# Later small loads, memory rows copied first, and a score bank and probability buffer per head in cross attention

## What is computed

```python
mods  = silu(c)     @ w_ada + b_ada          # shift and scale of the latent rows
cmods = silu(c_ctx) @ w_ada + b_ada          # the same for the context rows
h     = modulate(rmsnorm(x),   sh, sc)       # then h @ w_in: gates, keys, queries, values
h_ctx = modulate(rmsnorm(ctx), csh, csc)

m = rmsnorm(mem, mem_norm_g)                 # cross attention of the second block, 4 heads of 128
k, v = headnorm(m @ w_xk), m @ w_xv
q    = headnorm(rmsnorm(x, norm2_g) @ w_xq)
x    = x + softmax(q @ k.T * 128**-0.5) @ v @ w_xo
```

## Time and profile before

| | us |
|---|---|
| median of 3 runs | 1256.4 (1254.93 to 1256.63) |
| the profiled execution | 1256.11 |
| its span, first to last instruction | 1254.0 |
| TensorE busy | 1179.5 |
| VectorE busy | 409.3 |
| ScalarE busy | 321.7 |
| GpSimd busy | 30.5 |
| mean granted TensorE clock | 0.975 of full speed |

### The profile page before, as it was taken

The page is one execution under the profiler, slowest core; times in us unless marked ns, Lnnn a source line. Parts: engine busy times, 40 slices in busy tenths (PEclk is TensorE's granted clock), DMA queues, the critical chain, the costliest instruction groups (busy, mean ns, idle before and its releaser), DMA issues.

```text
span 1254.0 us, 16528 instructions
## 1 busy us (share of the span) xinstructions
PE 1179.5 (94%) x6732; PEld 874.2 (70%) x6732; DVE 409.3 (33%) x1018; ACT 321.7 (26%) x738; POOL 30.5 (2%) x54
## 2 busy tenths in 40 slices
PE   6999999999999989989999999889678979999997
PEld 5678888888878778765555555568556848887443
DVE  1424334212322221231111111216776422224545
ACT  2481010053422220142122111332554331000000
POOL 0000000000000011000000000032000000000000
PEclk9999999999999999999999999899879979999999
DMA  9923113213347873629999997534200404444530
GB/s 374 406 96 135 67 67 134 101 68 103 124 172 277 313 287 134 239 106 395 414 423 424 418 411 301 202 127 143 68 1 1 186 33 152 137 165 150 185 135 33
DMA packets 34361, 241.66 MB, mean 193 GB/s; under 512 B 3898, under 2 KB 4282, under 8 KB 6012
## 3 DMA queue, kind: packets, MB, share of 16 engines
q1 hardware_dynamic: 32640, 233.85, 47.7%
q10 hardware_dynamic: 1020, 4.06, 0.9%
q0 software_dynamic: 640, 2.90, 0.7%
HBM read 239.74 MB, written 1.05 MB: 192 GB/s over the span
## 4 chain that ended last, share of the span: by engine, by line
PE 87%; DVE 5%; ACT 3%; DMA 2%; issue 1%; SPq 1%; DVEq 0%; ACTq 0%
PE bank L1304 21%; PE bank L1331 11%; PE bank L1313 9%; PE bank L1694 9%; PE bank L2045 6%; PE bank L1717 5%; PE bank L1656 3%; PE bank L1665 3%; PE bank L1376 2%; DMA arena<-in_stream 2%; PE bank L1396 1%; PE bank L1566 1%; PE bank L1569 1%; PE bank L1514 1%; PE bank L2017 1%
## 5 line engine op out<-in xcount | busy, mean ns | idle before, releaser
L1304 PE MATMUL bank<-arena,ring 128*128 128x256 f32 x736 | 159.3, 379 | 0.0
L1304 PEld LDWEIGHTS bank<-arena,ring 128*128 128x128 f32 x736 | 139.8, 190 | 19.0
L1304 PE MATMUL bank<-hTl,ring 128*128 128x256 f32 x512 | 112.8, 379 | 0.0
L1304 PEld LDWEIGHTS bank<-hTl,ring 128*128 128x128 f32 x512 | 97.0, 190 | 16.9 <-issue 4.3
L691 ACT ACTIVATE arena<-bank 128x512 f32<-128x512 f32 x70 | 41.2, 601 | 235.9 <-PE bank L1304 211.4
L1331 PE MATMUL bank<-ring,arena 128*128 128x256 f32 x432 | 95.9, 379 | 1.0 <-ACT arena L1174 0.7
L1331 PEld LDWEIGHTS bank<-ring,arena 128*128 128x128 f32 x432 | 81.8, 190 | 12.6 <-ACT arena L1174 1.0
L1313 PE MATMUL bank<-ring,arena 128*128 128x256 f32 x384 | 86.6, 385 | 2.3 <-DVE arena L2354 2.2
L1313 PEld LDWEIGHTS bank<-ring,arena 128*128 128x128 f32 x384 | 73.6, 193 | 14.1 <-DVE arena L2354 2.6
L1694 PE MATMUL bank<-ring,arena 128*64 128x256 f32 x512 | 57.0, 381 | 0.0
L1313 PE MATMUL bank<-ring,hTl 128*128 128x256 f32 x256 | 56.9, 380 | 0.0
(11 more groups left out here) (503 smaller groups left out, 1684.9 us busy)
## 6 DMA issues: line engine op xcount, KB each, us to landing
ring<-in_stream SPq DMA_DIRECT2D x163, 1024.0 KB, 6.6
arena<-in_stream SPq DMA_DIRECT2D x38, 1024.0 KB, 9.0
hTl<-in_stream SPq DMA_DIRECT2D x9, 1024.0 KB, 7.8
hTc<-in_stream SPq DMA_DIRECT2D x9, 1024.0 KB, 9.8
consts<-in_consts ACTq DMA_DIRECT2D x1, 2697.0 KB, 13.7
arena<-in_mem SPq DMA_DIRECT2D x1, 1024.0 KB, 8.1
arena<-in_x SPq DMA_DIRECT2D x1, 1024.0 KB, 22.2
arena<-in_ctx SPq DMA_DIRECT2D x1, 1024.0 KB, 24.2
```

The lines of the kernel that those rows point to most:

```text
L1304: mm = pe.matmul(b[:, 256 * n:256 * n + 256], w[:, k, 128 * n:128 * n + 128], h[:, k, :], start=(k == 0), stop=(k == KD - 1))
```

## The change

In the first stage: only the identity is loaded at the start, the other six tables go with the late load of `consts`, for which TensorE now waits ahead of the products that use them. `cols` moves from third on ScalarE's queue to first on SyncE's. `wr`, `wukv` and `rows` move to GpSimd's queue behind the second modulation (`adaT_ready` 2). `wlr` moves from ScalarE's queue to SyncE's, between ring tiles 4 and 5, behind a wait for the first modulation. ScalarE copies the memory rows before its two Silu and the `preload`, which now reads the identity in place of `ones`.

In cross attention: scores of head n go to `bank[4 + n]`, four banks; T(n) goes to two of the lower four banks and AV(n) to the other two; `xP` has four buffers, in a part of the arena that is free then. TensorE makes scores 2 and 3 right after `xqT1`; VectorE takes all four maxima before W(0); ScalarE's order is written out; AV(2) and AV(3) wait for the copy of AV(0) and AV(1).

```diff
--- before.py
+++ after.py
@@ -431,7 +431,7 @@
         qx, qxT = region(22528, NT, 512), region(23552, XH, L)
-        xP = [region(24576, 512), region(25088, 512)]
+        xP = [region(LC + 512 * n, 512) for n in range(XH)]
         xPT = [region(25600, 512), region(26112, 512)]
@@ -542,6 +542,7 @@
+            sp.dma_start(cols[:, :], coldram).then_inc(cols_in, 16)
             sp.dma_start(memx, mem.rearrange("b (i p) d -> p (b i) d", p=P)).then_inc(mem_in, 16)
@@ -556,6 +557,10 @@
                     load_ada(1)
+                elif t == 5:
+                    sp.wait_ge(ada_ready, 1)
+                    sp.dma_start(wlr[0:65, :], wlr_d[:, 0:1024]).then_inc(own_in, 16)
+                    sp.dma_start(wlr_own[0:65, :], wlr_d[:, 1024:2048]).then_inc(own_in, 16)
                 load(t)
@@ -615,11 +620,14 @@
         def _(pool):
-            pool.dma_start(rows[:, :], rowdram.partition_broadcast(P)).then_inc(rows_in, 16)
             pool.memset(sc32, 0.0).then_inc(sc_zero, 1)
             pool.memset(lrT[64:65, :], 1.0).then_inc(lr_ones, 1)
+            pool.wait_ge(adaT_ready, 2)
+            pool.dma_start(wr[:, :], wr_d).then_inc(small_in, 16)
+            pool.dma_start(wukv[:, :], wukv_d).then_inc(small_in, 16)
+            pool.dma_start(rows[:, :], rowdram.partition_broadcast(P)).then_inc(rows_in, 16)
             pool.wait_ge(sum_ready, NO["fac3"] + 1)
@@ -674,11 +682,8 @@
             step = Count()
-            act.dma_start(consts[:, 0:7 * P], cdram[:, 0:7 * P]).then_inc(tables_in, 16)
+            act.dma_start(consts[:, 0:P], cdram[:, 0:P]).then_inc(tables_in, 16)
             act.dma_start(cv[:, :], cvec).then_inc(cv_in, 16)
-            act.dma_start(cols[:, :], coldram).then_inc(cols_in, 16)
-            act.dma_start(wr[:, :], wr_d).then_inc(small_in, 16)
-            act.dma_start(wukv[:, :], wukv_d).then_inc(small_in, 16)
             taken = Count()
@@ -700,10 +705,6 @@
-            act.wait_ge(cv_in, 16)
-            act.activation(sc[:, :], cv[:, :], ACT.Silu).then_inc(sc_ready, 1)
-            act.wait_ge(sc_zero, 1)
-            act.activation(sc32[:, :, 0:2], cv[:, :].rearrange("p (k c) -> p k c", c=2), ACT.Silu).then_inc(sc_ready, 1)
             sq = Count()
@@ -711,7 +712,7 @@
                 n = loads.one() - 1
-                act.activation(warm[:, n:n + 1], ones[:, 0:1], func)
+                act.activation(warm[:, n:n + 1], ident[:, 0:1], func)
@@ -720,7 +721,6 @@
-            preload(ACT.Sqrt)
             act.wait_ge(cols_in, 16)
@@ -728,6 +728,11 @@
                 ins.then_inc(raw_act, 1)
+            act.wait_ge(cv_in, 16)
+            act.activation(sc[:, :], cv[:, :], ACT.Silu).then_inc(sc_ready, 1)
+            act.wait_ge(sc_zero, 1)
+            act.activation(sc32[:, :, 0:2], cv[:, :].rearrange("p (k c) -> p k c", c=2), ACT.Silu).then_inc(sc_ready, 1)
+            preload(ACT.Sqrt)
             row_squares(memx, 2, junk0)
@@ -745,8 +750,6 @@
             act.activation(ada_rows[:, 0:256], bank[4][:, 0:256], ACT.Copy).then_inc(rows_ready, 1)
-            act.dma_start(wlr[0:65, :], wlr_d[:, 0:1024]).then_inc(own_in, 16)
-            act.dma_start(wlr_own[0:65, :], wlr_d[:, 1024:2048]).then_inc(own_in, 16)
             act.wait_ge(head_ms, 1)
@@ -760,7 +763,7 @@
-            act.dma_start(consts[:, 7 * P:], cdram[:, 7 * P:]).then_inc(consts_in, 16)
+            act.dma_start(consts[:, P:], cdram[:, P:]).then_inc(consts_in, 16)
             act.wait_ge(mod_ready, 2)
@@ -1236,20 +1239,31 @@
             preload(ACT.Exp)
-            for n in range(XH + 1):
-                if n < XH:
-                    act.wait_ge(s_max, STEPS + n + 1)
-                    for i in range(NT):
-                        act.activation(xP[n % 2][:, 256 * i:256 * i + 256], bank[4 + n % 2][:, 256 * i:256 * i + 256], ACT.Exp,
-                                       scale=qfac[:, 4 * i + n:4 * i + n + 1], bias=smx[:, 2 * n + i:2 * n + i + 1],
-                                       accum_out=ssum[:, 2 * n + i:2 * n + i + 1]).then_inc((act_step, probs)[i], 1)
-                    step.one()
-                m = n - 1
-                if m >= 0:
-                    act.wait_ge(pt_ready, 2 * STEPS + 4 + m + 1)
-                    if m >= 2:
-                        act.wait_ge(av_done, 2 * STEPS + m - 1)
-                    act.activation(xPT[m % 2], bank[6 + m % 2][:, :], ACT.Copy).then_inc(pt_taken, 1)
+
+            def query_exps(n):
+
+                act.wait_ge(s_max, STEPS + n + 1)
+                for i in range(NT):
+                    act.activation(xP[n][:, 256 * i:256 * i + 256], bank[4 + n][:, 256 * i:256 * i + 256], ACT.Exp,
+                                   scale=qfac[:, 4 * i + n:4 * i + n + 1], bias=smx[:, 2 * n + i:2 * n + i + 1],
+                                   accum_out=ssum[:, 2 * n + i:2 * n + i + 1]).then_inc((act_step, probs)[i], 1)
+                step.one()
+
+            def query_turned(m):
+
+                act.wait_ge(pt_ready, 2 * STEPS + 4 + m + 1)
+                if m >= 2:
+                    act.wait_ge(av_done, 2 * STEPS + m - 1)
+                act.activation(xPT[m % 2], bank[(NO["xp00"] + 2 + m % 2) % NB][:, :], ACT.Copy).then_inc(pt_taken, 1)
+
+            query_exps(0)
+            query_exps(1)
+            query_turned(0)
+            query_exps(2)
+            query_turned(1)
+            query_exps(3)
+            query_turned(2)
+            query_turned(3)
             preload(ACT.Sqrt)
@@ -1484,6 +1498,7 @@
             pe.wait_ge(la_ready, 8)
+            pe.wait_ge(consts_in, 16)
             after, before = C("after"), C("before")
@@ -1972,10 +1987,8 @@
-                if n >= 2:
-                    pe.wait_ge(probs, STEPS + n - 1)
                 for j in range(NT):
-                    mm = pe.matmul(bank[4 + n % 2][:, 256 * j:256 * j + 256], qxT[:, n, 128 * j:128 * j + 128],
+                    mm = pe.matmul(bank[4 + n][:, 256 * j:256 * j + 256], qxT[:, n, 128 * j:128 * j + 128],
                                    kxT[:, n, :], start=True, stop=True)
@@ -1985,25 +1998,26 @@
             pe.wait_ge(sum_taken, NO["xqT1"] + 1)
-            for n in range(1, XH + 2):
-                if 2 <= n < XH:
-                    query_scores(n)
-                m = n - 1
-                if 0 <= m < XH:
-                    pe.wait_ge(pair_norm, STEPS + m + 1)
-                    if m >= 2:
-                        pe.wait_ge(pt_taken, 2 * STEPS + 4 + m - 1)
+            query_scores(2)
+            query_scores(3)
+            for n in range(XH + 1):
+                if n < XH:
+                    pe.wait_ge(pair_norm, STEPS + n + 1)
+                    if n >= 2:
+                        pe.wait_ge(pt_taken, 2 * STEPS + 4 + n - 1)
                     for c in range(2):
                         for j in range(NT):
-                            mm = pe.transpose(bank[6 + m % 2][:, 256 * c + 128 * j:256 * c + 128 * j + 128],
-                                              xP[m % 2][:, 256 * j + 128 * c:256 * j + 128 * c + 128], ident)
+                            mm = pe.transpose(bank[(NO["xp00"] + 2 + n % 2) % NB][:, 256 * c + 128 * j:256 * c + 128 * j + 128],
+                                              xP[n][:, 256 * j + 128 * c:256 * j + 128 * c + 128], ident)
                     mm.then_inc(pt_ready, 1)
-                m = n - 2
+                m = n - 1
                 if m >= 0:
+                    if m >= 2:
+                        pe.wait_ge(ox_ready, m - 1)
                     pe.wait_ge(pt_taken, 2 * STEPS + 4 + m + 1)
                     for c in range(2):
-                        mm = pe.matmul(bank[(NO["xp00"] + m) % NB][:, 0:256], vx[:, c, XD * m:XD * m + XD], xPT[m % 2][:, 256 * c:256 * c + 256],
-                                       start=(c == 0), stop=(c == 1))
+                        mm = pe.matmul(bank[(NO["xp00"] + m % 2) % NB][:, 0:256], vx[:, c, XD * m:XD * m + XD],
+                                       xPT[m % 2][:, 256 * c:256 * c + 256], start=(c == 0), stop=(c == 1))
                     mm.then_inc(av_done, 1)
@@ -2903,7 +2917,7 @@
                 dve.wait_ge(s_ready, 2 * STEPS + n + 1)
-                T(dve.tensor_reduce(smx[:, 2 * n:2 * n + 2], bank[4 + n % 2][:, :].rearrange("p (i m) -> p i m", i=NT),
+                T(dve.tensor_reduce(smx[:, 2 * n:2 * n + 2], bank[4 + n][:, :].rearrange("p (i m) -> p i m", i=NT),
                                     AX.X, ALU.max, negate=True))
@@ -2917,14 +2931,14 @@
                 for i in range(NT):
-                    pr = xP[n % 2][:, 256 * i:256 * i + 256]
+                    pr = xP[n][:, 256 * i:256 * i + 256]
                     ins = dve.tensor_scalar(pr, pr, ssum[:, 2 * n + i:2 * n + i + 1], None, ALU.mult)
                 dve.wait_ge(av_done, 2 * STEPS + m + 1)
-                dve.tensor_copy(oxT[:, m, :], bank[(NO["xp00"] + m) % NB][:, 0:256]).then_inc(ox_ready, 1)
```

(5 more changed lines are left out.)

## The result

| | before | after |
|---|---|---|
| median, us | 1256.5 (4 runs) | 1244.7 (1243.2 to 1246.6, 4 runs) |
| profiled execution, us | 1256.1 | 1245.5 |
| second modulation starts (L1418, now L1432) | 44.6 | 40.9 |
| ScalarE's copy of `xqT1` starts | 1002.5 | 1000.3 |
| projection on the chain | 1024.75 | 1013.87 |

The ratio is 0.9904 with a 95% interval of 0.989 to 0.9917: 11.8 us faster, where 7.2 were forecast, and 0.3 us outside the range. The table says where: 3.7 us are won at the start, 2.2 are left at cross attention, and cross attention gives 8.6 to 8.7 more.

A forecast was written before the change was run, and what follows sets the result against it. TensorE, carrying 87% of the chain, was taken as the bound, so only its waits and slow stretches count. Start 3.0 plus cross attention 4.2 gave 7.2 us off, forecast 1249.2 us, 8-in-10 range 1245.0 to 1252.8.

The forecast's parts named there:

- I take mostly low, with half a round's saving: 4.2: Cross attention: TensorE's clock mostly low, gain 3.4 us, raised by half a round's saving to 4.2 us.
- The working for each clock: Cross attention, step by step to the projection: gain 3.4 us at TensorE's low clock, 8.1 us at the full one.
- rival (c): Cross attention: the clock stays full throughout, gain 8.1 us, total time 1245.3 us; chance 0.14.
- The start: First stage up to the second modulation: 3.0 us earlier, bounds 1.3 to 4.0 us.
- tile 2 and the products meet at `xv0`: Start: TensorE reaches `xv0` at 28.6 to 30.9 us, ring tile 2 lands at 31.3; gain there 1.9 us.
- the memory rows' 7.2: Start: memory rows, with fewer loads sharing the DMA engines, arrive at 7.2 us instead of 8.94.
- the first product's 10.9: Start: TensorE's first product begins at about 10.9 us instead of 13.20, 2.3 us earlier.
- Tile 2 was put at 31.3: Start: 0.82 MB removed ahead of ring tile 2 brings it 1.9 us earlier, from 33.2 to 31.3 us.
- the last `w_ada` tile was put at 41.4: Start: tile for the second modulation lands at 41.4 us, from 44.6 less 1.9 and 1.3 for moving `wlr`.
- `cols` in its place: Start: `cols` first in its queue adds no bytes, is no longer last, and delays the memory rows 0.2 us.
- The worst case for tile 5: After the start: late small loads take all bandwidth, tile 5 lands by 59.5 us, needed at 60.4; nothing charged.
- Rival (a): Start: loads are hidden anyway, time comes back at a later tile, only cross attention pays; 1252.2 us, chance 0.12.

The follow-up runs named there:

- filled: Kernel before, with useless products added where TensorE would wait in cross attention, and nothing of the change: 1251.3 us, ratio 0.9967.
- start_only: Kernel before with only the first-stage part of the change, cross attention as before: 1253.6 us, ratio 0.9971.
- scores_late: Changed kernel with scores 2 and 3 back behind T(0), and their maxima behind W(0) and W(1): 1247.3 us, ratio to before 0.9925.
- smalls_early: Changed kernel with `rows`, `wr` and `wukv` issued at the start again: 1247.9 us, ratio to before 0.9927.
- cols_act: Changed kernel with `cols` issued by ScalarE behind `cv`, not first by SyncE: 1247.7 us, ratio to before 0.9929.
- after_again: The changed kernel, unaltered, measured once more beside later versions on the same chip: 1242.8 us, ratio to before 0.9895.
- the version with both edits: Changed kernel with VectorE's weightings 2 and 3 each ahead of copies 0 and 1, and ring tile 2 issued ahead of `x` and `ctx`: 1239.3 us.
- weights_first: Changed kernel with VectorE's order W(2), copy 0, W(3), copy 1 instead of copy 0, W(2), copy 1, W(3): 1243.4 us, ratio to before 0.9893.
- wlr_act: Changed kernel with `wlr` issued by ScalarE behind the first modulation again: 1245.3 us, ratio to before 0.9903.
- cross_only: Kernel before with only the cross-attention part of the change, start as before: 1248.3 us, ratio 0.9937.
- tables_early: Changed kernel with all seven small tables of `consts` loaded at the start again, 384 KB more: 1243.5 us, ratio to before 0.9903.

## Why the prediction was too small

**The step that failed** is "I take mostly low, with half a round's saving: 4.2" in cross attention. The working for each clock was good: 8.1 was forecast for the full one and 8.6 came. I chose the wrong one of the two, from an average busy share and one pair of windows. By then the clock had already been at 0.50 once, right behind the longest wait, and the same working had shortened that wait from 4.44 us to 2.6 (1004.9 to 1007.5; 1.88 came). The "half a round" that lifts 3.4 to 4.2 rests on no row. What the runs put in its place: at the full clock the order gives 3.6, and the clock 5.0 of its own (filled; 3.3 by the profile of start_only); with the long wait back, the clock falls behind it (scores_late). This was rival (c), with a chance of 0.14; it should have had most of it. The traces speak for it: behind 4.44 us (before) and 4.43 us (scores_late) the clock fell to 0.50, and the waits of 1.24 us between the rounds of the changed kernel left it at 1.00.

**The start** was forecast 3.0 and was 3.7 in the profiles at the second modulation, 2.9 to 3.6 alone in the runs. The mechanism was right that tile 2 and the products meet at `xv0`, and the memory rows' 7.2 (7.06), the first product's 10.9 (10.5) and the hidden table load held. Two terms were mis-sized. Tile 2 was put at 31.3 by bytes alone; it came at 29.7. Of the 1.6 us between, an estimate of 0.9 is the slow stretch, 240 GB/s instead of 424 over 2 us, which comes with `rows`, `wr` and `wukv` (smalls_early); the rest is not resolved. And the last `w_ada` tile was put at 41.4, of which 1.3 us for `wlr`; it landed near 39.3, and TensorE, there at 40.9, did not wait for it, so what bound the second modulation was the chain behind tile 2. The term that I gave no price of its own, `cols` in its place, decides as much as all bytes (cols_act). The worst case for tile 5 did not come; it was not waited for.

**The sum.** Rival (a) fell: the gain of the start comes through. But not whole. From the second modulation to `xqT1` TensorE does the same work in 957.6 us before, 959.1 in after, 956.6 in after_again, and the mean granted clock of the whole execution was 0.977 in after and 0.981 in after_again. That these differences are the clock at stalls in the middle is read from the traces, not tested by an edit. The traces show it at single waits, such as this one of the kernel before, and the same wait in the changed kernel, each with a window behind it:

```profile
442.81 0.33 PE L1597 MATMUL bank<-consts,hTc 128*128 128x128 f32 x1 [3.81 <-DVE arena L2329]
...
444.00:446.00 2.00, 1.93 (x17) 1.53 (x15) 1.54 (x4) 2.00 (x6) 0.00 (x0) 1.00 1.03 434
```

```profile
439.07 0.48 PE L1612 MATMUL bank<-consts,hTc 128*128 128x128 f32 x1 [3.81 <-DVE arena L2343]
...
440.00:442.00 2.00, 2.00 (x11) 2.00 (x10) 1.40 (x4) 1.75 (x5) 0.00 (x0) 0.50 1.06 446
```

The wait is as long in both, and only one of them lost the clock; after_again lost it there too, the version with both edits did not. This is the size of what the prediction could not size, and it can hide a gain of 1.6 us like that of weights_first.

## What to carry to other kernels

Where TensorE works in short pieces and its granted clock falls behind a wait, as here to 0.50 behind 4.44 us, cost the pieces at both clocks and look at the longest wait, not only at the mean busy share: filling the waits with useless work was worth 4.1 to 5.1 us here (filled). Waits of 2 to 4 us cut both ways here: the one of 2.20 us between 503 and 512 us lost the clock in six of the fourteen profiles, the one of 3.8 between 437 and 445 in twelve. So a gain of 1 or 2 us elsewhere can come and go with them. Where a start follows a full DMA stream, price the place of each small load as well as its bytes: one 80 KB load behind others on a second queue cost 3.0 us (cols_act), about all that the start had gained. Where two things are moved in one stage, undo each alone before calling either useless: here either one, put back, took nearly the whole gain of the start (3.2 us in smalls_early, 3.0 in cols_act).

## What the runs showed of the hardware

- Useless TensorE work in the waits of cross attention made the kernel faster (ratio 0.9967, 0.9952 to 0.9981; filled).
- The same 32 instructions of `xv0` took 7.17 us behind waits up to 1.72 us (filled), 8.7 to 8.9 behind 2.0 to 2.5 (weights_first, wlr_act, start_only), and 9.87 behind 3.56 (smalls_early); the slow ones have windows of 2 us at a granted clock of 0.50 to 0.66 in them.
- Length alone does not decide: the same wait of 3.8 us, near 440, lost the clock in twelve of the fourteen profiles, and not in the kernel before and the version with both edits (granted clock 0.50 in after from 440 to 442, 1.00 in before from 444 to 446). Of the waits of 4.3 to 5.0 us between 20 and 1010 us, 45 in the fourteen profiles, every one did (4.44 in before, 4.43 in scores_late).
- With `rows`, `wr` and `wukv` in flight the DMA engines were 0.86 to 1.01 busy and moved 216 to 269 GB/s between 6 and 8 us (cross_only, filled, before, smalls_early); with the 448 KB of tables instead, 3.5 KB per partition, 444 (tables_early). Which of the three does it stays open: no run here separated the length of their rows from the queue that issued them.
- A load of 79.5 KB took 2.3 us as the first of its queue and 9.9 as the third of another, at the same start of the kernel.
